# Dilated attention and last norm: ScalarE takes a unit's exponents before its copies, and the norm's output is made by token tile

## The reference, cut to what matters

```
# layer 1, per group (window, dilation) = (128,1), (512,4), (2048,16), 8 heads of 64
s = q.k / 8 - slope[h] * dist * dilation;  s = -1e30 where not valid
m = max(s);  e = exp(s - m);  den = sum(e);  o = e @ v
o = sum_g o_g * exp(m_g - M) / sum_g den_g * exp(m_g - M)
# ... output projection, residual, MLP, residual ...
y = x * rsqrt(mean(x*x) + 1e-6) * norm_final        # per token, 1024 wide
```

## Time and profile before

| what | value |
|---|---|
| median of 3 runs | 1749.65 us (1745.19 to 1749.69) |
| profiled execution, own time | 1754.7 us |
| its span | 1752.9 us |
| TensorE busy | 88% of the span |
| VectorE, ScalarE, POOL busy | 41%, 26%, 35% |
| mean granted TensorE clock | 0.924 |
| last residual to the end of the span | 1720.7 to 1752.9 us |

### The profile page before, as it was taken

The page is one execution under the profiler, slowest core; times in us unless marked ns, Lnnn a source line. Parts: engine busy times, 40 slices in busy tenths (PEclk is TensorE's granted clock), DMA queues, the critical chain, the costliest instruction groups (busy, mean ns, idle before and its releaser), DMA issues.

```text
span 1752.9 us, 28109 instructions
## 1 busy us (share of the span) xinstructions
PE 1536.0 (88%) x12025; PEld 1404.4 (80%) x12025; DVE 712.9 (41%) x1014; ACT 464.5 (26%) x872; POOL 610.6 (35%) x276
## 2 busy tenths in 40 slices
PE   6878875788899999999999989987659999999995
PEld 6755544455699899998999989975529989999894
DVE  4767752787254300341132563133356430034014
ACT  4224442243332211222221111024414221122210
POOL 2311103243236634564334333220013653366340
PEclk9989995899899999999999989887769999999997
DMA  4276305476243544453425554549401543544211
GB/s 142 68 241 238 97 1 190 166 285 249 73 145 125 188 145 173 139 191 121 144 73 194 168 200 152 177 148 325 145 0 49 186 150 120 191 137 177 95 48 49
DMA packets 123322, 258.53 MB, mean 147 GB/s; under 512 B 7088, under 2 KB 104512, under 8 KB 116896
## 3 DMA queue, kind: packets, MB, share of 16 engines
q1 hardware_dynamic: 117088, 219.49, 36.5%
q0 software_dynamic: 6144, 37.75, 5.8%
HBM read 249.62 MB, written 95.58 MB: 197 GB/s over the span
## 4 chain that ended last, share of the span: by engine, by line
PE 79%; DVE 11%; ACT 3%; issue 2%; DMA 2%; POOL 1%; SPq 0%; DVEq 0%; POOLq 0%; ACTq 0%
PE ps L488 20%; PE ps L492 20%; PE ps L489 20%; PE ps L747 4%; PE ps L654 2%; PE ps L766 1%; DVE sq L1557 1%; PE ps L691 1%; PE ps L885 1%; PE ps L928 1%; PE ps L665 1%; ACT sc L2048 1%; DMA dv<-q_scratch 1%; PE ps L848 1%; PE ps L988 1%
## 5 line engine op out<-in xcount | busy, mean ns | idle before, releaser
L2090 POOL TENSOR_TENSOR whl<-wraw,whl 128x2048 fp32r<-128x2048 f32 (+3 forms) x127 | 446.6, 3525 | 603.0 <-ACT whl L1763 603.0
L488 PE MATMUL ps<-hA,whl 128*128 128x260 f32 x1248 | 337.9, 291 | 19.6 <-POOL hA L2090 13.8
L489 PE MATMUL ps<-hA,whl 128*128 128x260 f32 x1248 | 333.0, 287 | 0.0
L1763 ACT ACTIVATE whl<-wraw 128x2048 fp32r<-128x2048 f32 (+3 forms) x127 | 185.9, 1484 | 482.2 <-PE ps L492 414.0
L488 PE MATMUL ps<-uT,whl 128*128 128x260 f32 x1024 | 273.2, 287 | 16.8 <-POOL uT L2090 16.8
L489 PE MATMUL ps<-uT,whl 128*128 128x260 f32 x1024 | 270.7, 285 | 0.0
L488 PEld LDWEIGHTS ps<-hA,whl 128*128 128x128 f32 x1248 | 242.1, 194 | 21.7 <-POOL hA L2090 15.4
L492 PE MATMUL ps<-hA,whl 128*128 128x260 f32 x1248 | 256.4, 287 | 0.0
L489 PEld LDWEIGHTS ps<-hA,whl 128*128 128x128 f32 x1248 | 242.5, 194 | 0.1
L488 PEld LDWEIGHTS ps<-uT,whl 128*128 128x128 f32 x1024 | 196.3, 192 | 17.6 <-issue 17.6
L492 PE MATMUL ps<-uT,whl 128*128 128x260 f32 x1024 | 209.2, 286 | 0.0
(11 more groups left out here) (284 smaller groups left out, 2047.7 us busy)
## 6 DMA issues: line engine op xcount, KB each, us to landing
out_ds<-in_state SPq DMA_DIRECT2D x32, 2047.0 KB, 10.4
wraw<-in_w_up SPq DMA_DIRECT2D x32, 1024.0 KB, 5.6
wraw<-in_w_down SPq DMA_DIRECT2D x32, 1024.0 KB, 5.1
wraw<-in_w_qkv SPq DMA_DIRECT2D x18, 1024.0 KB, 6.9
out_ds<-in_state SPq DMA_DIRECT2D x8, 2044.0 KB, 13.0
dv<-in_state SPq DMA_DIRECT2D x36, 256.0 KB, 6.6
dv<-q_scratch SPq DMA_DIRECT2D x6, 1024.0 KB, 7.2
wraw<-in_w_omla SPq DMA_DIRECT2D x4, 1024.0 KB, 5.1
```

Source lines behind the costliest of these rows:

```text
L488: pe.matmul(ps[:, 2 * u + a, 0:HALF], hi(k), rhs(k, 0)[:, c], start=first, stop=False)
L489: pe.matmul(ps[:, 2 * u + a, 0:HALF], hi(k), rhs(k, 1)[:, c], start=False, stop=False)
L1763: ins = act.activation(dst(0), src, ACT.Copy)
L2090: return pool.tensor_tensor(dst, src, hi.bitcast(F32), ALU.subtract)
```

## The change

In the dilated loop ScalarE now takes all exponents of unit k and then the four copies of unit k, where it went back and forth between the copies of k-1 and the exponents of k. In the last norm, ScalarE writes `xg` = `xT` times the gain of each feature during the last down projection (one more instruction per feature tile, after the square). TensorE sums the squares per token: five matmuls with a block of tokens as the stationary operand and one column of ones, which puts the sums of 128 tokens on 128 partitions, 5 columns in all. The root is made on these 128x5. TensorE turns `xg` (not yet scaled) by token tile, eight transposes for each of tiles 0, 1, 2, samples, 3, into PSUM units 1, 2, 3, 0, 1. The scaling by the token's root happens in the copy out of PSUM: VectorE takes tiles 0, 2 and the samples, ScalarE tiles 1 and 3. SP stores each tile when it is copied, with five DMAs.

```
@@ TensorE, the end
-            u = z_begin()
-            square_total(u)
-            ...
-            for f in range(DT):
-                pe.wait_ge(final_ready, f + 1)
-                ... four transposes of tmp[:, f % 4] and one of the samples
+            pe.wait_ge(tile_taken, vw.at("tile_summed"))
+            pe.wait_ge(squares_added, (DT - 1) * vw.tick("sums"))
+            for t in range(NB_T + 1):
+                tok = slice(0, P) if t == NB_T else slice(NS + t * P, NS + (t + 1) * P)
+                ins = pe.matmul(ps[:, 0, t:t + 1], square_sum[:, tok], ones[:, 0:1], start=True, stop=True, skip_group_check=True)
+            ins.then_inc(token_sums_ready, 1)
+            pe.wait_ge(final_ready, DT)
+            for t in FINAL:
+                ...
+                if t == NB_T:
+                    pe.wait_ge(token_sums_taken, 1)
+                elif t == 3:
+                    pe.wait_ge(rows_copied_dve, 1)
+                u = FINAL_UNIT[t]
+                for f in range(DT):
+                    ins = pe.transpose(ps[0:n, 2 * u + f // 4, (f % 4) * P:(f % 4 + 1) * P], xg[:, f, tok], ident[:])
+                ins.then_inc(rows_turned, 1)
@@ SP, the end
-            sp.wait_ge(tile_taken, mark["last"])
-            sp.dma_start(io["yp"]..., yn[:, 0:NB_T, :]).then_inc(rows_stored, 16)
-            sp.dma_start(io["ys"], yn[0:NS, NB_T, :]).then_inc(rows_stored, 16)
+            for t in FINAL:
+                who = "act" if t in (1, 3) else "dve"
+                done[who] += 1
+                sp.wait_ge(rows_copied_act if who == "act" else rows_copied_dve, done[who])
+                ... one dma_start of tile t
@@ VectorE, the end
-            rsqrt(D)
-            ... final(f), copies by feature tile
+            dve.wait_ge(token_sums_ready, 1)
+            dve.tensor_scalar(token_mean, ps[:, 0, 0:NB_T + 1], 1.0 / D, EPS, ALU.mult, ALU.add).then_inc(token_sums_taken, 1)
+            dve.wait_ge(token_sums_taken, 1)
+            dve.reciprocal(token_inverse, token_mean).then_inc(inverse_ready, 1)
+            dve.wait_ge(root_ready, vw.tick("root_ready"))
+            ... the Newton step: two linked instructions and a third into token_root, then token_root_ready
+            for i, t in enumerate(FINAL):
+                if t in (1, 3):
+                    continue
+                dve.wait_ge(rows_turned, i + 1)
+                dve.tensor_scalar(yn[0:n, t, :]..., ps[0:n, 2 * FINAL_UNIT[t]:2 * FINAL_UNIT[t] + 2, :],
+                                  token_root[0:n, t:t + 1], None, ALU.mult).then_inc(rows_copied_dve, 1)
@@ ScalarE, last down projection
                             if not last:
                                 norm_hi(f, 2 * DT, h_mix)
+                            else:
+                                act.activation(xg[:, f, :], xT[:, f, :], ACT.Copy,
+                                               scale=gains[:, 4 * DT + f:4 * DT + f + 1]).then_inc(final_ready, 1)
@@ ScalarE, dilated loop
-            for k in range(DU + 1):
+            for k in range(DU):
                 for j in range(4):
-                    if k:
-                        d_taken(k - 1, j)
-                    if k < DU:
-                        d_exp(k, j)
+                    d_exp(k, j)
+                for j in range(4):
+                    d_taken(k, j)
@@ ScalarE, the end
+            act.wait_ge(inverse_ready, vw.tick("inverse_ready"))
+            act.activation(token_root, token_inverse, ACT.Sqrt).then_inc(root_ready, 1)
+            act.wait_ge(token_root_ready, 1)
+            for i, t in enumerate(FINAL):
+                if t in (1, 3):
+                    act.wait_ge(rows_turned, i + 1)
+                    act.activation(yn[:, t, :]..., ps[:, 2 * FINAL_UNIT[t]:2 * FINAL_UNIT[t] + 2, :],
+                                   ACT.Copy, scale=token_root[:, t:t + 1]).then_inc(rows_copied_act, 1)
```

More of the change, by code:

```diff
@@ L211, in program @@
         cx = ExitStack()
+        xg = sb("xg", [P, DT, T], F32, cx)
+        cx.close()
+        cx = ExitStack()
         sc = sb("sc", [P, 3, 2, 8 * P], F32, cx)
@@ L244, in program @@
         square_sum = sq[:, 0, :]
+        FINAL = (0, 1, 2, NB_T, 3)
+        FINAL_UNIT = {0: 1, 1: 2, 2: 3, NB_T: 0, 3: 1}
+        token_mean, token_inverse, token_root = (tmp[:, i, 0:NB_T + 1] for i in range(3))
         squared = [rstd[:], sq[:, 1, :]]
@@ L358, in program @@
         final_ready = semaphore("final_ready")
+        token_sums_ready = semaphore("token_sums_ready")
+        token_sums_taken = semaphore("token_sums_taken")
+        token_root_ready = semaphore("token_root_ready")
+        rows_turned = semaphore("rows_turned")
+        rows_copied_dve = semaphore("rows_copied_dve")
+        rows_copied_act = semaphore("rows_copied_act")
         dve_step = semaphore("dve_step")
@@ L994, in _ @@
             mlp()
-            u = z_begin()
-            square_total(u)
-            vw.tick("tile_summed")
-            for f in range(DT):
-                pe.wait_ge(final_ready, f + 1)
[L1001 to L1005, removed]
+            pe.wait_ge(tile_taken, vw.at("tile_summed"))
[6 more added lines that the diff above has]
+            for t in FINAL:
+                n = NS if t == NB_T else P
+                tok = slice(0, NS) if t == NB_T else slice(NS + t * P, NS + (t + 1) * P)
+                if t == NB_T:
[6 more added lines that the diff above has]
+                ins.then_inc(rows_turned, 1)
         @block.sync
@@ L1728, in _ @@
             mlp(last=True)
-            rsqrt(D)
             dve.wait_ge(tile_low, vw.at("a"))
[L1733 to L1743, removed]
+            dve.wait_ge(token_sums_ready, 1)
[3 more added lines that the diff above has]
+            dve.wait_ge(root_ready, vw.tick("root_ready"))
+            link(dve.scalar_tensor_tensor(out=token_inverse, in0=token_root, scalar=-0.5, in1=token_root, op0=ALU.mult, op1=ALU.mult))
+            link(dve.tensor_tensor(token_inverse, token_inverse, token_mean, ALU.mult))
+            dve.scalar_tensor_tensor(out=token_root, in0=token_inverse, scalar=1.5, in1=token_root, op0=ALU.add,
+                                     op1=ALU.mult).then_inc(token_root_ready, 1)
+            dve.wait_ge(token_root_ready, 1)
+            for i, t in enumerate(FINAL):
+                if t in (1, 3):
+                    continue
+                n = NS if t == NB_T else P
+                dve.wait_ge(rows_turned, i + 1)
+                dve.tensor_scalar(yn[0:n, t, :].rearrange("p (a n) -> p a n", a=2), ps[0:n, 2 * FINAL_UNIT[t]:2 * FINAL_UNIT[t] + 2, :],
+                                  token_root[0:n, t:t + 1], None, ALU.mult).then_inc(rows_copied_dve, 1)
         @block.scalar
```

11 lines of the change are left out of this document (7 added, 4 removed).

## The result

The changed kernel takes **1706.97 us** (median of four runs, 1706.1 to 1708.9), the kernel before 1749.31 beside it (four runs). The ratio is 0.9765, 95% interval 0.9747 to 0.9782: the change saves 42 us, where 53.4 were forecast. The time lies inside the forecast range of 1690 to 1708, at its upper end, 10.8 above the predicted 1696.2.

The account below looks back on a forecast made before the run. The dilated loop was held by engines waiting for each other, not by one engine. Loop gain 37.9 plus tail gain 15.5 made 53.4 us, taken from the median 1749.65: 1696.2 us, range 1690 to 1708.

Parts of the forecast that it names:

- The bound and the mechanism: Dilated loop: copies queued behind an exponent waiting for maxima; reordering takes a pair from 27.5 to 15.4 us, gain 37.9.
- What binds next is ScalarE: Dilated loop after the change: ScalarE's exponents and copies would bind, at 15.4 us a pair.
- odd ones half of 4.1, so 2.1: Dilated loop: odd units' scores would take 2.1 us at full clock, half of the profiled 4.1.
- falls here followed 2.36 us or more, so I take full clock: Dilated loop: TensorE's longest idle stretch would be 1.7 us, under the 2.36 seen before a fall, so 2.4 GHz throughout.
- the prediction's own recurrence: Dilated loop: unit-by-unit sum of scores, maxima, exponents, copies and values; 15.4 us a pair, unit 7 ending at 1236.4.
- Rival 1: Dilated loop: the clock stays low in the scores (3.3 and 4.1 us); gain 30.5 + 15.5, 1703.7 us; chance 0.18.
- Rival 4: Tail: five stores run one behind the other, 3.7 us each, 2.5 the small one; tail gain 7.4, 1704.4 us; chance 0.07.
- Rival 2: Dilated loop: the clock stays low throughout, values and transposes slow too; gain 13 + 14, 1722.6 us; chance 0.06.
- Rival 3: After the dilated loop: its gain is given back by late weights, only the tail's is left; 1734 us; chance 0.04.
- Rival 5: Dilated loop: scores of k+1 run only after values of k, each unit serial at 20.1 us; 1780 us; chance 0.02.
- The tail: Last norm to the end: smaller root, earlier transposes and stores by tile; gain 16.6 to 14.0 us, taken as 15.5.
- its own test: Wrong if the dilated loop ends later than 1244 on the old scale, or the stretch to the output projection grows.

Follow-up runs that it names:

- early transposes: The changed kernel with the transposes of features 0 to 6 of the first two token tiles put before the row sums: 1704.93 us (ratio 0.9733).
- one store: The changed kernel with its final rows stored as before, one store of 2 MB and one of 32 KB behind all copies: 1709.99 us (ratio 0.9766).
- the version with everything: The changed kernel plus side-by-side operands for odd scores, by-block ScalarE order in odd units and tail transposes ahead of the row sums: 1693.60 us (ratio 0.9665).

## Why the prediction was right or wrong

- **The bound and the mechanism: right.** The loop was held by the exponent that stood ahead of three copies. With the order alone changed, a pair fell from 27.5 to between 16.2 and 18.6. One sentence of it does not follow from its own terms: "What binds next is ScalarE". ScalarE's work of a pair sums to 14.6 (3.8, 3.1, 4.0, 3.7), and the odd unit's path, from the end of one odd unit's values to the next one's, to 15.2 (scores 2.1, maxima 4.7, exponents 4.0, values 4.4). In the trace ScalarE does wait for the maxima of units 3, 5 and 7, some 1.05 us each time. The 4.7 is 4.9 by the earlier trace rows, from 1204.1 to 1209.0.
- **"odd ones half of 4.1, so 2.1": the step that failed.** It took the 4.1 of the earlier trace rows for a low-clock time, as the even scores' 3.3 was. But they take 4.12 at 1.00 too, because of the step in their operands. The trace before could have told it. These are its windows in the first odd scores, which begin at 1172.6, and their matmuls seen by source line, ahead of the fall and behind it:

```profile
1173.00:1174.00 1.00, 1.00 (x12) 1.00 (x12) 1.00 (x3) 0.00 (x0) 0.00 (x0) 0.85 1.82 655
1174.00:1175.00 1.00, 1.00 (x12) 1.00 (x12) 0.74 (x3) 0.19 (x1) 0.00 (x0) 0.50 1.14 393
...
L928 PE MATMUL ps<-dk,dq x7: 412/412/596, 1172.6 to 1173.5; 64*128 64x128 f32 x7
...
L928 PE MATMUL ps<-dk,dq x16: 412/414/415, 1173.7 to 1175.4; 64*128 64x128 f32 x16
```

  As many records stand in a microsecond at 0.50 as at 0.85, and one takes 412 ns at 1.00 and 414 at 0.50: the clock had no part in their time. With 4.1 at full clock the prediction's own recurrence gives 4.1 scores, 4.7 maxima, 4.0 exponents and 4.4 to the values' end: 17.2 a pair instead of 15.4, and unit 7 ends at 1241.8 on the old scale, that of the profile before, whose loop starts 2.9 us later. That is a gain of 32.5, so this term was mis-sized by 5.4. Without a fall a pair takes 17.3 in a trace (1195.92 to 1213.26, early transposes).
- **"falls here followed 2.36 us or more, so I take full clock": failed too.** The shortest idle stretch that a fall had followed was taken for a bound, though that is no more than the shortest case seen. The longest idle stretch was foreseen well (1.7, measured 1.79), and falls followed it. The rest of the miss, 32.5 less 27.7, is 4.8 us; two falls take 2.5 of it (78.1 against 75.6) and the third, at unit 7's values, 1.9. The 0.4 that are left are about what the 4.7 in place of 4.9 gives over three odd units.
- **Rivals 1 and 4** gave 1703.7 and 1704.4 and stand nearest to the time, but neither by its mechanism. Rival 1 put the low clock into the scores, and from unit 2 on those ran at 1.00; only "4.1 for odd scores" is common to it and the runs. **Rival 2** didn't come: values of even units stayed at 0.66.
- **Rival 3, the gain given back: wrong, as argued.** From the last values to the first matmul of the output projection it was 36.4 us before (1274.26 to 1310.67) and 36.4 after (1243.66 to 1280.08).
- **Rival 4, stores one behind the other: wrong.** The stores were issued at 1698.80, 1700.32, 1702.00, 1703.18 (the samples) and 1703.57, where it took each to need 3.7 us by itself; the end is 3.6 us behind the last copy (3.7 forecast), with one store 7.6. So what the Trainium skill says in "DMA: Bandwidth & Descriptors", section "Bandwidth", of transfers of 1 MiB and more did not decide here: pieces of 512 KB moved at 373 and 344 GB/s in the windows above, beside copies that a single store would have waited for.
- **Rival 5, slower: wrong**; the scores of k+1 ran ahead of the transposes of k, as the code says.
- **The tail: right in sum, 16.2 against 15.5**, and in its steps from the last residual on: row sums done after 4.4 us (forecast 4.4), the root after 5.7 (6.0), the last copy after 12.4 (11.9 to 14.5), the end after 15.9 (15.6 to 18.2). The 40 transposes took 6.8 because the clock rose only between 1700 and 1701. The xg copies took 0.71 each instead of 0.64 and hid as forecast.
- The text named its own test: wrong if the loop ends later than 1244 on the old scale. It ended at 1243.66 + 2.9 = 1246.6, so by its own test the prediction failed, although the time fell into its range.

## What to carry to other kernels

Before a duration is halved for a better clock, look whether the same operation stands at full clock anywhere in the trace, and compare its weight loads: those of the strided fp32 operand here take 0.33 us at either clock, and those of side-by-side tokens 0.33 at 0.50 and 0.19 at 1.00. Put instructions of an in-order engine in the order in which their inputs come ready, block by block where a whole unit ahead leaves the next engine idle; count that idle stretch as a risk to TensorE's clock, and work the time out both with a fall and without one. Cut a last store along the work that makes it, until the transfer itself is the bound.

## What was not expected of the hardware

- A step of 16 bytes in either fp32 operand of a matmul costs about the same as in both: 3.90 and 4.03 against 4.12 us, and 2.06 with none. At 1.00 the strided weight load takes 0.33 us, the other 0.19.
- The granted clock fell to 0.50 after idle stretches of 1.79 and 1.70 us, and in other executions of the same loop it didn't after the same 1.79. In the version with everything it fell at 1229, where the last longer idle stretch was one of 1.43 us.
- Transposes alone brought the clock back: from 1695.6 on TensorE did nothing else, and PEclk went from 0.50 to 1.00 between 1700 and 1701; as filler in the loop they went with 1.00 in the values of units 3 and 5. The Trainium skill, "TensorE: Matmul & The Clock Gate", section "Part 4: PE-mode transpose", says that the full clock doesn't engage for them. The measurement decides: for these fp32 transposes it does.
